# Matmuls of the identity from the start, and a new order of the first transposes, in a one-core decoder layer

## The reference, cut to what matters

```python
def rmsnorm(x, w):
    xf = x.astype(jnp.float32)
    y = xf * lax.rsqrt(jnp.mean(xf * xf, axis=-1, keepdims=True) + RMS_EPS)
    return (y * w.astype(jnp.float32)).astype(x.dtype)
...
    xn = rmsnorm(x, ln1_w)
    z = xn @ w_in
```

## Time and profile before

| | |
|---|---|
| median of 3 runs | 712.95 us (712.56 to 714.05) |
| span of the profiled execution | 712.2 us |
| instructions | 15199 |
| TensorE busy | 688.5 us (97%) |
| VectorE, ScalarE, GpSimd busy | 452.0, 296.1, 313.4 us |

### The profile page before, as it was taken

One profiled execution on the slowest core, in us unless ns is written; L12 is line 12 of the kernel. 1 busy time (PEld: TensorE's weight loads), 2 busy tenths in 40 slices (PEclk: granted clock), 3 DMA queues, 4 the chain that ended last, 5 costly groups with the idle time before them and its releaser, 6 DMA issues.

```text
span 712.2 us, 15199 instructions
## 1 busy us (share of the span) xinstructions
PE 688.5 (97%) x5563; PEld 642.0 (90%) x5563; DVE 452.0 (63%) x894; ACT 296.1 (42%) x568; POOL 313.4 (44%) x229
## 2 busy tenths in 40 slices
PE   6989899999999999999998999999999999999996
PEld 6988778869777777899998999999999999999996
DVE  4497989885342537637688784856748567575133
ACT  6242644545352213236555435244353444334222
POOL 6227998923222244245427707144080431606531
PEclk9999999999999999999999999999999999999999
DMA  7727898844765869743203323313133232423103
GB/s 242 236 84 199 273 295 253 256 125 119 226 198 155 261 187 289 124 148 92 88 1 107 112 79 119 120 60 119 59 118 118 76 101 62 152 84 119 60 1 121
DMA packets 88633, 100.41 MB, mean 141 GB/s; under 512 B 5374, under 2 KB 64338, under 8 KB 88570
## 3 DMA queue, kind: packets, MB, share of 16 engines
q1 hardware_dynamic: 74566, 92.91, 42.1%
q10 hardware_dynamic: 14004, 6.67, 4.1%
HBM read 92.92 MB, written 6.64 MB: 140 GB/s over the span
## 4 chain that ended last, share of the span: by engine, by line
PE 76%; DVE 11%; ACT 4%; issue 3%; POOL 3%; DMA 1%; ACTq 0%; SPq 0%; DVEq 0%; POOLq 0%
PE acc L895 6%; PE acc L896 6%; PE acc L897 6%; PE acc L1399 5%; PE acc L1398 5%; PE acc L1400 5%; PE acc L1364 4%; PE acc L1366 4%; PE acc L1365 4%; PE scr L1399 3%; PE scr L1400 3%; PE scr L1398 3%; PE scr L1364 3%; PE scr L1365 3%; PE scr L1366 3%
## 5 line engine op out<-in xcount | busy, mean ns | idle before, releaser
L895 PE MATMUL acc<-act_hi,w_hi 128*128 128x256 f32 (+1 forms) x416 | 122.0, 293 | 1.2 <-DVE zT L2476 1.2
L1994 POOL TENSOR_TENSOR h_lo<-relu,h_hi 128x520 fp32r<-128x520 f32 x32 | 44.8, 1400 | 167.8 <-ACT h_hi L1785 167.2
L896 PE MATMUL acc<-act_lo,w_hi 128*128 128x256 f32 (+1 forms) x416 | 117.4, 282 | 0.0
L897 PE MATMUL acc<-act_hi,w_lo 128*128 128x256 f32 (+1 forms) x416 | 117.2, 282 | 0.0
L1949 POOL TENSOR_TENSOR prod<-kv,Qb 128x1024 f32<-128x1024 f32 x32 | 85.8, 2716 | 33.6 <-DVE S L2178 17.3
L1484 POOL TENSOR_TENSOR w_lo<-raw,w_hi 128x1024 fp32r<-128x1024 f32 x20 | 47.7, 2386 | 98.0 <-ACT w_hi L1477 98.0
L895 PEld LDWEIGHTS acc<-act_hi,w_hi 128*128 128x128 f32 x416 | 78.3, 188 | 7.2 <-issue 5.0
L896 PEld LDWEIGHTS acc<-act_lo,w_hi 128*128 128x128 f32 x416 | 78.5, 189 | 0.0
L897 PEld LDWEIGHTS acc<-act_hi,w_lo 128*128 128x128 f32 x416 | 78.3, 188 | 0.0
L2495 DVE TENSOR_TENSOR xT<-acc,xT 128x260 f32<-128x260 f32 x64 | 26.3, 425 | 55.1 <-PE acc L1400 55.1
L2476 DVE TENSOR_TENSOR zT<-acc,rstd 128x264 f32<-128x264 f32 (+1 forms) x56 | 23.5, 422 | 49.2 <-PE acc L897 46.6
(11 more groups left out here) (422 smaller groups left out, 2310.9 us busy)
## 6 DMA issues: line engine op xcount, KB each, us to landing
kv<-in_cache_k_dram SPq DMA_DIRECT2D x64, 256.0 KB, 3.5
kv<-in_cache_v_dram SPq DMA_DIRECT2D x64, 256.0 KB, 3.2
raw<-in_w_up_dram SPq DMA_DIRECT2D x16, 1024.0 KB, 5.5
raw_d<-in_w_down_dram SPq DMA_DIRECT2D x12, 1024.0 KB, 5.1
raw<-in_w_in_dram SPq DMA_DIRECT2D x14, 512.0 KB, 5.8
raw<-in_w_in_dram SPq DMA_DIRECT2D x7, 1024.0 KB, 7.5
x_tok<-in_x_prompt_dram SPq DMA_DIRECT2D x8, 512.0 KB, 5.4
raw<-in_w_out_dram SPq DMA_DIRECT2D x4, 1024.0 KB, 7.8
```

Source lines behind the costliest of these rows:

```text
L895: pe.matmul(out, w_hi[:, slot, k, :], hi[k][:, cols], start=(n == 0), stop=False)
L896: pe.matmul(out, w_hi[:, slot, k, :], lo[k][:, cols], start=False, stop=False)
L897: mm = pe.matmul(out, w_lo[:, slot, k, :], hi[k][:, cols], start=False, stop=(n == KT - 1))
L1994: pool.tensor_tensor(h_lo[:, t, :], relu2[:, t % 2, :], h_hi[:, t, :].bitcast(F32), ALU.subtract).then_inc(s_hs_lo, 1)
```

## The change

It does five things.

1. The identity is made first on GpSimd: its select stands behind one memset instead of behind seven, and `s_ident_ok` now counts this alone (`even` has a semaphore of its own, on which only a much later job waits).
2. TensorE starts with 8 matmuls of the identity by itself into a bank nobody reads (`WARM = 8`).
3. TensorE's order behind them is: samples, tile 2 for all four jobs, norm weights, tile 3 for all four jobs. A job `x1` n is complete with its second transpose of tile 3. Before, it was: norm weights, samples, and tiles 2 and 3 job by job.
4. On ScalarE the sums of squares of tiles 2 and 3 stand behind all eight `act_hi` and behind `w_hi` of tile 1; on GpSimd `w_lo` of tile 1 stands ahead of 1/rms.
5. Norm weights and samples use banks of `acc` and semaphores of their own, so the jobs `param` and `xs` are gone and every later job number is lower by two.

```diff
-    job("param", 0)
-    job("xs", 0)
...
-            pe.wait_ge(s_ident_ok, 3)
-            out = open_job(pe, "param", 0)
-            pe.wait_ge(s_ln1_in, 16)
-            done(pe.transpose(out[:, 0:KT], ln1_rows[:, :], ident[0:KT, 0:KT]))
-            out = open_job(pe, "xs", 0)
+            def early_tile(c, i):
+
+                pe.wait_ge(x_in[i], 16)
+                for n in range(4):
+                    out = bank("x1", n) if c else open_job(pe, "x1", n)
+                    for j in (2 * n, 2 * n + 1):
+                        col = (j % 2) * SPLIT_TOK + c * P
+                        mm = pe.transpose(out[:, col:col + P], x_tok[:, i, j * P:(j + 1) * P], ident[:, :])
+                    if c:
+                        done(mm)
+
+            pe.wait_ge(s_ident_ok, 1)
+            for _ in range(WARM):
+                pe.matmul(acc[:, 3, 0:P], ident[:, :], ident[:, :], start=True, stop=True)
             pe.wait_ge(x_in[NT], 16)
             for j in range(KT):
-                mm = pe.transpose(out[:, j * NS:(j + 1) * NS], x_s[:, j * P:(j + 1) * P], ident[0:NS, 0:NS])
-            done(mm)
-            for n in range(4):
-                x_to_cols(("x1", n), n, (2, 3))
+                mm = pe.transpose(acc[:, 2, j * NS:(j + 1) * NS], x_s[:, j * P:(j + 1) * P], ident[0:NS, 0:NS])
+            mm.then_inc(s_xs_up, 1)
+            early_tile(0, 2)
+            pe.wait_ge(s_ln1_in, 16)
+            pe.transpose(acc[:, 1, 0:KT], ln1_rows[:, :], ident[0:KT, 0:KT]).then_inc(s_ln1_up, 1)
+            early_tile(1, 3)
...
-            out = full(act, "param", 0)
-            free(act.activation(par[:, 0:KT], out[:, 0:KT], ACT.Copy), "param", 0)
-            square_sum(2)
-            out = full(act, "xs", 0)
-            free(act.activation(xn_s[:, :, :].rearrange("p j b -> p (j b)"), out[:, 0:KT * NS], ACT.Copy), "xs", 0)
-            evacuated(act, "param", 0)
+            act.wait_ge(s_xs_up, 1)
+            act.activation(xn_s[:, :, :].rearrange("p j b -> p (j b)"), acc[:, 2, 0:KT * NS], ACT.Copy)\
+               .then_inc(s_xs_copied, 1)
+            act.wait_ge(s_ln1_up, 1)
+            act.activation(par[:, 0:KT], acc[:, 1, 0:KT], ACT.Copy).then_inc(s_ln1_ok, 1)
+            act.wait_ge(s_ln1_ok, 1)
             for n in range(4):
                 x_hi(("x1", n), n, 1)
                 if n == 1:
                     split(0)
+            split(1)
+            square_sum(2)
             square_sum(3)
-            split(1)
             split(2)
...
             pool.memset(ident[:, :], 0.0).then_inc(s_pool_chain, 1)
+            pool.wait_ge(s_pool_chain, 1)
+            pool.affine_select(out=ident[:, :], in_=ident[:, :], compare_op=ALU.not_equal, fill=1.0, base=0,
+                               pattern=[[-1, P]], channel_multiplier=1).then_inc(s_ident_ok, 1)
             pool.memset(causal[:, :], 0.0).then_inc(s_pool_chain, 1)
...
             weight_lo(pool, 0, 0, 0)
+            weight_lo(pool, 1, 1, 0)
             pool.wait_ge(s_x_ms_ok, 2)
             rsqrt(rs[:, 2:NT], P, 2).then_inc(s_x_rs_ok, 1)
             rsqrt(rs[0:NS, NT:NT + 1], NS, 1).then_inc(s_x_rs_ok, 1)
-            weight_lo(pool, 1, 1, 0)
             weight_lo(pool, 2, 2, 1)
...
-            dve.wait_ge(s_ident_ok, 3)
+            dve.wait_ge(s_ident_ok, 1)
...
-            evacuated(dve, "param", 0)
+            dve.wait_ge(s_ln1_ok, 1)
...
-            evacuated(dve, "xs", 0)
+            dve.wait_ge(s_xs_copied, 1)
```

More of the change, by code:

```diff
@@ L63 @@
 AHEAD = 3
+WARM = 8
 POOL_LO = 20
@@ L567, in build @@
         s_ident_ok = sem("ident_ok")
+        s_even_ok = sem("even_ok")
+        s_ln1_up = sem("ln1_up")
+        s_ln1_ok = sem("ln1_ok")
+        s_xs_up = sem("xs_up")
+        s_xs_copied = sem("xs_copied")
         s_causal_ok = sem("causal_ok")
@@ L1160, in task @@
                     pe.wait_ge(s_samp_dve, 2)
+                    pe.wait_ge(s_even_ok, 2)
                     out = open_job(pe, "own", 0)
@@ L1910, in _ @@
             pool.wait_ge(s_pool_chain, 5)
-            pool.affine_select(out=ident[:, :], in_=ident[:, :], compare_op=ALU.not_equal, fill=1.0, base=0,
-                               pattern=[[-1, P]], channel_multiplier=1).then_inc(s_ident_ok, 1)
             pool.affine_select(out=causal[:, SEQ - P:SEQ], in_=causal[:, SEQ - P:SEQ], compare_op=ALU.is_ge,
@@ L1917, in _ @@
             pool.affine_select(out=even[:, 0:1], in_=even[:, 0:1], compare_op=ALU.is_ge, fill=1.0, base=-64,
-                               pattern=[[1, 1]], channel_multiplier=1).then_inc(s_ident_ok, 1)
+                               pattern=[[1, 1]], channel_multiplier=1).then_inc(s_even_ok, 1)
             pool.affine_select(out=even[:, 1:2], in_=even[:, 1:2], compare_op=ALU.is_ge, fill=1.0, base=63,
-                               pattern=[[1, 1]], channel_multiplier=-1).then_inc(s_ident_ok, 1)
+                               pattern=[[1, 1]], channel_multiplier=-1).then_inc(s_even_ok, 1)
             for rows_split in (qs_split, M_split):
```

## The result

The changed kernel is slower by about 0.2%: **715.35 us** median of 20 runs (713.83 to 717.28), against 713.08 us (712.43 to 715.56) in 20 runs of the kernel before on the same chip. The ratio is 1.0023, 95% interval 1.0014 to 1.0032. (The ratios of this document are worked out from all runs; they are not the quotients of the two medians, which would be 1.0032 here.) The forecast was 712.5 us, with a range of 711.2 to 714.1. Two executions far outside all others, 2375.02 us of `e7_after_all_fill` and 1349.06 us of the kernel before beside it, are left out of the ratios.

The account below looks back on a forecast made before the run. TensorE, 97% busy, was taken as the bound, with the front set by ScalarE's first `act_hi`. An `act_hi` 0.4 us earlier, all else costing 0, gave 712.95 - 0.4 = 712.5 us, range 711.2 to 714.1.

Parts of the forecast that it names:

- What bounds the kernel: Whole span: TensorE is busy 97%, so a shift of its work at the start should travel to the end.
- The base: Whole kernel: the runs' median, 712.95 us, stood 0.75 us above the profiled span of 712.2.
- Identity first and the warm-up: Kernel start: TensorE starts at 1.45 instead of 5.34 us; 16 cold records take 3.47 us, to 4.92.
- When does the clock rise? Two rows bound it: Front, TensorE: full clock comes 3.4 to 5.1 us after the first instruction, at 4.85 or 6.6 us.
- cold all the way: Rival, front: clock rises only behind tile 3, `act_hi` up to 0.75 us later; 713.1 to 713.7 us, chance 0.15.
- The new order: Front, TensorE: ten transposes instead of four ahead of the first `act_hi`; all cold, 8.33 us, 0.75 later than 7.58.
- -0.4: Front: first `act_hi` starts 0.4 us earlier, middle of 6.8 to 7.6 us, bounds -0.8 and +0.75.
- The fallback rival: Ahead of projection: about 2.0 us idle drops the clock; 713.2 to 714.2 partly hidden (0.15), 714.65 in full (0.07).
- The sum: Whole kernel: span 712.2 - 0.4 = 711.8 us, median 712.95 - 0.4 = 712.5 us.
- Squares, GpSimd's order, SyncE, banks: Front, other engines: moved squares, `w_lo` ahead of 1/rms, SyncE's page loads and two fewer jobs each cost 0.
- Something else shifts: Rival, near 379 us: the earlier start happens to spare the clock fall at 379.10; 710.8 us, chance 0.13.

Follow-up runs that it names:

- e7_after_all_fill: Changed kernel plus nine identity matmuls behind tile 3's transposes and identity matmuls in the waits at 71 and 376 us; 714.76 us, ratio 1.0012.
- e11: The changed kernel as it is, profiled once more, one run; 717.31 us.
- e4: Changed kernel with the squares of tiles 2 and 3 and GpSimd's 1/rms back in their old places; 715.83 us, ratio 1.0026.
- e1: Changed kernel plus nine identity matmuls behind tile 3's transposes, filling the idle stretch ahead of the projection; 714.4 us, ratio 1.0017.
- e5: Kernel before, front untouched, plus ten identity matmuls in the wait at 71 us and eight at 376 us; 712.54 us, ratio 0.9984.
- e10: Changed kernel, front untouched, plus identity matmuls in the waits at 71 and 376 us; 715.33 us, ratio 1.0027.
- e12: The changed kernel as it is, profiled again, one run; 713.92 us.
- e6: Kernel before with identity first, eight identity matmuls ahead, six behind tiles 2 and 3's transposes, and the waits at 71 and 376 us filled; 713.34 us, ratio 0.9999.
- e3: Kernel before with the identity made first and eight identity matmuls ahead of its own order of transposes; 713.66 us, ratio 0.9994.
- e8: Changed kernel with TensorE's old order of transposes, keeping warm-up, banks, semaphores and new place of the squares; 714.07 us, ratio 1.0005.

## Why the prediction was wrong, step by step

- **What bounds the kernel: right.** A shift in the front travels to the end: 1.5 us in the first profile from 28 to 400 us, 3.1 us in e11, 2.8 in e4.
- **The base: wrong.** I took 0.75 us between span and median. It is 1.7 to 1.8 for every run of this kernel; the profiled execution carried a fall that the median, it seems, did not. I had the row (379.10) and did not draw this.
- **Identity first and the warm-up: nearly right.** TensorE starts at 1.60 instead of 1.45; the 16 records take 3.79 us instead of 3.47; so 5.39 instead of 4.92. The samples take 0.72 where the warm sum had 0.43. These two make `act_hi` late, 7.76, although the rise at 5.66 lay inside my two bounds. Even with the rise at 4.73, in e1, it starts at 7.37, where I gave 6.8.
- **"When does the clock rise? Two rows bound it": this step failed.** 3.4 to 5.1 us behind the first instruction was no bound. The profiles with the warm-up show 3.1, 4.0, 4.1, 3.8, 4.4, 4.4 and 2.9, and 8.4, 9.6 and 15.9 in e4, e7 and e11, although TensorE has no gap up to 10.2 (in e11 an idle stretch of 1.44 us follows then, and the rise comes after it). So the rise came before 6.1 us or not before 9.9. The transposes behind the burst do not by themselves keep it away: in e5 the clock rose at 9.87 with nothing but transposes since 5.50. With a late rise the ten transposes ahead of the first `act_hi` are cold: 9.15, where I gave 8.33 as the worst. I put "cold all the way" at +0.75 and "all same"; it is +1.57 at `act_hi` and up to 3.3 us at the end, since the first projection tiles are cold as well.
- **The new order: the sign was seen, its weight not.** I wrote that "the reorder alone is a loss; what pays for it is the clock". The clock pays in one form only, and then just back to 7.37 to 7.76; my -0.4 did not come.
- **The fallback rival: the mechanism and the raw price right, its chance and its discounts wrong.** The idle stretch of about 2.0 us is 2.06; the fall follows in three of three early-form profiles of this front (first profile, e10, e12). I gave it 0.22 and let waits hide up to 0.5 and the early start another 0.4. The price is 1.3 to 1.5 us, as the raw 1.2 to 1.7 said, and nothing hid it. The sum itself had no term for it: its last pair was to start at 12.3, and started at 12.93, inside the half clock.
- **Squares, GpSimd's order, SyncE, banks: right, cost 0** (e4 against the changed kernel; `w_hi` of tile 2 at 15.16 instead of 15.21).
- **"Something else shifts": right that it happens, wrong as a gain for this change.** The fall at 379 was spared in the first profile. It is there or not in either kernel.

Two steps failed. One is the rise of the clock, and with it the term of -0.4: `act_hi` was to come between 6.8 and 7.6, 8.33 at worst, and came at 7.37 to 7.76 or at 9.15. The other is the fall behind the idle stretch, which the sum left out and the rival discounted. What the runs put in their place: either the rise is early and the hole brings a fall, or it is late and everything starts 1.5 us late. No run of 22 was under 713.8, where the kernel before has half of its first 20 runs below 713.1.

What stays open: why the rise sometimes comes 8 us and more behind the first identity matmul; why in e6 and e10 up to 2.9 us lie between span and time; and where the tail up to 719 us in e1, e7 and e10 comes from. In e1 the three runs above 716 have low granted clocks (0.992, 0.992 and 0.989), in e7 the two above 716 do not (0.996), and the profile of e10 shows a long DMA issue. How often each of the two forms occurs among the 20 runs is not shown either.

## What to carry to other kernels

Work that keeps TensorE warm must at least reach without a gap to the real work, and even then it has to be timed: filled up to the projection, e1 and e6 were no faster than the kernel before. A burst followed by a wait of 2 us bought a fall of the clock, while the same kind of matmuls laid into the waits of the unchanged kernel took 0.0011 to 0.0016 off its time in two comparisons. Do not lengthen what stands ahead of the first useful result on the strength of a clock that must rise in time; count the path at the lower clock. And where times stand in groups 1.5 us apart, look in which group the profiled execution lies before its span is used as a base.

## What the runs showed of the hardware

- The granted clock fell for 3.41 us at a time behind idle stretches of 1.20 us (the fall at 54 us in e3, e5, e6, and the one at 56 in e7) to 2.06 us, not behind each: 1.20 near 52 us was followed by no fall in the other ten profiles, 1.40 by a fall in e8 and by none in e3_before_warm.
- A fall of 6.83 us occurs as well, in e1_fill; it began 2.1 us into an idle stretch of 2.3 us, which was followed by none in the profiles of both kernels.
- Not every fall costs time: those at 54 us were made good within 50 us, those in the first projection (the changed kernel, e10, e12) were not.
- The profile prints 1.00 for the clock before the first record; the pace of the matmuls (27 records in 6.03 us) is the only sign of the lower level there.
- The Trainium skill, page "TensorE: Matmul & The Clock Gate", section "What's actually happening", says that the point of transition varies by 500 ns either way from run to run, and that one should not fit to a count. The profiles agree that it moves, and by far more: the same eight matmuls were followed by a rise 2.9 to 15.9 us after their start.
